# Expert down matrices loaded as four neighbouring rows per partition, in a two-block transformer kernel

## The reference, cut to what matters

```python
def expert_choice_moe(h, w_router, w1, w3, w2):
    ...
    xg = h[bidx, idx]                                  # 16 experts x 32 tokens x 1024
    h1 = jnp.einsum('becd,edf->becf', xg, w1)          # w1, w3, w2: 16 x 1024 x 1024, per layer
    h3 = jnp.einsum('becd,edf->becf', xg, w3)
    out = jnp.einsum('becf,efd->becd', jax.nn.silu(h1) * h3, w2)
    out = out * vals.astype(h.dtype)[..., None]
    return jnp.zeros_like(h).at[bidx, idx].add(out)
```

## Time and profile before

| | |
|---|---|
| median of 3 runs | 1896.9 us (1896.03 to 1896.99) |
| the profiled execution, its own time | 1900.6 us |
| its span | 1898.8 us |
| PE busy | 1550.6 us, 82% |
| PE weight loads, DVE, ACT, POOL busy | 60%, 32%, 26%, 10% |
| moved by DMA | 563.65 MB, mean 297 GB/s |
| chain that ended last | PE 52%, DMA 36% (all of it expert matrices) |

### The profile page before, as it was taken

One profiled execution on the slowest core, in us unless ns is written; L12 is line 12 of the kernel. 1 busy time (PEld: TensorE's weight loads), 2 busy tenths in 40 slices (PEclk: granted clock), 3 DMA queues, 4 the chain that ended last, 5 costly groups with the idle time before them and its releaser, 6 DMA issues.

```text
span 1898.8 us, 29516 instructions
## 1 busy us (share of the span) xinstructions
PE 1550.6 (82%) x12506; PEld 1135.1 (60%) x12506; DVE 612.3 (32%) x923; ACT 500.4 (26%) x910; POOL 193.9 (10%) x214
## 2 busy tenths in 40 slices
PE   7999999999999999665655656999998666666656
PEld 6999899998898886232322323997883322323225
DVE  3456534577556353000000002655450000000005
ACT  3433333556444432000000002454330000000003
POOL 0043000011041100000000002410100000000003
PEclk9999999999999999898888888999999888989888
DMA  8564549432554569999999999545399999999994
GB/s 284 164 219 168 195 155 301 152 111 91 178 172 136 177 233 386 425 427 424 427 426 424 427 426 377 180 152 178 128 378 394 426 425 424 427 425 427 426 425 152
DMA packets 166894, 563.65 MB, mean 297 GB/s; under 512 B 10559, under 2 KB 120027, under 8 KB 133896
## 3 DMA queue, kind: packets, MB, share of 16 engines
q1 hardware_dynamic: 159012, 552.08, 75.1%
q10 hardware_dynamic: 7780, 10.10, 1.6%
HBM read 561.08 MB, written 5.23 MB: 298 GB/s over the span
## 4 chain that ended last, share of the span: by engine, by line
PE 52%; DMA 36%; DVE 4%; ACT 3%; issue 3%; POOL 1%; SPq 0%; ACTq 0%; DVEq 0%; POOLq 0%
DMA ring<-in_moe_w 36%; PE bank L965 21%; PE bank L1213 7%; PE bank L1622 5%; PE bank L921 4%; PE bank L1060 3%; PE bank L1645 2%; PE bank L1276 2%; ACT ring_r L1695 1%; ACT big L1743 1%; PE bank L1090 1%; PE bank L1480 1%; PE bank L1285 1%; PE bank L1037 1%; PE bank L1651 1%
## 5 line engine op out<-in xcount | busy, mean ns | idle before, releaser
L1622 PE MATMUL bank<-ring,big 128*32 128x256 f32 x3840 | 281.3, 443 | 195.7 <-DMA ring<-in_moe_w 193.2
L1622 PEld LDWEIGHTS bank<-ring,big 128*32 128x32 f32 x3840 | 147.0, 123 | 335.8 <-issue 295.4
L965 PE MATMUL bank<-big_r,ring_r 128*128 128x256 f32 (+1 forms) x2760 | 344.1, 285 | 0.0
L965 PEld LDWEIGHTS bank<-big_r,ring_r 128*128 128x128 f32 (+1 forms) x2760 | 335.1, 191 | 3.0 <-issue 2.2
L2092 DVE TENSOR_TENSOR ring_r<-ring,ring_r 128x2048 fp32r<-128x2048 f32 (+2 forms) x105 | 243.0, 2319 | 135.3 <-ACT ring_r L1695 133.9
L1743 ACT ACTIVATE big<-bank 128x512 f32<-128x512 f32 (+2 forms) x186 | 87.9, 491 | 571.6 <-PE bank L921 366.8
L1695 ACT ACTIVATE ring_r<-ring 128x2048 fp32r<-128x2048 f32 (+2 forms) x109 | 204.2, 1881 | 10.4 <-DMA ring<-in_ev_w_out 5.1
L1645 PE MATMUL bank<-ring,big 128*32 128x512 f32 x1024 | 136.7, 634 | 74.0 <-DMA ring<-in_moe_w 55.5
L2479 DVE SCALAR_TENSOR_TENSOR big<-big,bank 128x256 f32<-128x256 f32 x32 | 13.5, 421 | 463.9 <-ACT big L1995 463.9
L1213 PE MATMUL bank<-ring_r,big_r 128*128 128x512 f32 x576 | 135.7, 395 | 0.7 <-DVE big_r L2099 0.7
L921 PE MATMUL bank<-big 128*128 128x128 f32 (+6 forms) x636 | 105.1, 292 | 35.7 <-ACT big L1743 18.2
(11 more groups left out here) (204 smaller groups left out, 1512.8 us busy)
## 6 DMA issues: line engine op xcount, KB each, us to landing
ring<-in_moe_w SPq DMA_DIRECT2D x120, 2048.0 KB, 23.7
ring<-in_moe_w SPq DMA_DIRECT2D x128, 1024.0 KB, 24.9
ring<-in_w_in SPq DMA_DIRECT2D x28, 1024.0 KB, 5.4
ring<-in_od_w_in SPq DMA_DIRECT2D x22, 1024.0 KB, 6.5
ring<-in_ev_w_in SPq DMA_DIRECT2D x20, 1024.0 KB, 7.3
big<-in_moe_w SPq DMA_DIRECT2D x8, 2048.0 KB, 11.2
ring<-in_ev_w_out SPq DMA_DIRECT2D x8, 1024.0 KB, 5.0
ring<-in_od_cmp_w SPq DMA_DIRECT2D x8, 1024.0 KB, 8.1
```

What stands on the lines that cost most here:

```text
L965: ins = unit[0].mark(mm(dst, lhsT, rhs, start=start and n == 0, stop=stop and n == len(terms) - 1))
L1622: ins = mm(banks[5 + up][32 * j:32 * j + 32, 0:256], xg[:, k, q, :], wv[:, r, 256 * j:256 * (j + 1)], start=k == 0, stop=k == KC - 1)
```

## The change

The down matrix of an expert is now loaded like the up matrices, in two loads of 2 MiB with 16 KB per partition. In the last expert of each batch the second of these is cut in two loads of 1 MiB, each with two neighbouring rows (8 KB) of every partition (`deep_half`). The down product takes two units, or three for that expert; its matmuls stay 16 (32 instructions), in another order. For the rows of a partition to meet their inner features, each of the four column groups of an up product now takes every fourth inner feature (`cols`) and not a block of 256 in a row, and VectorE writes `mb` straight through. Bytes, numbers of matmuls and the slots per expert stay as they are.

```diff
--- before.py
+++ after.py
@@ -784,6 +784,13 @@
                 src = flat(m)[bass.ds(row, per * P), :].rearrange("(p r) c -> p (r c)", r=per)
                 sp.dma_start(ring[:, s * SLOT:s * SLOT + per * D], src).then_inc(units_in[s], 16)
 
+            def deep_half(m, row, h):
+
+                s, rnd, n = w.next()
+                sp.wait_ge(begun, n - RING + 2 + (rnd - n // RING - 1) * RING)
+                src = flat(m)[bass.ds(row, 4 * P), :].rearrange("(p r) c -> p (r c)", r=4)
+                sp.dma_start(ring[:, s * SLOT:s * SLOT + 2 * D], src[:, 2 * D * h:2 * D * (h + 1)]).then_inc(units_in[s], 16)
+
             for l in range(LAYERS):
                 for unit in LAYER_UNITS:
                     name, i = unit[0], unit[1]
@@ -809,15 +816,19 @@
                     src = flat(ups[i % 2])[row:row + 4 * P, :].rearrange("(p r) c -> p (r c)", r=4)
                     sp.dma_start(view(spare_at[i], P, 4 * D), src).then_inc(spare_in[i], 16)
 
-                def down(row):
-                    for i in range(4):
-                        deep(a["moe_w2_2"], row + 256 * i, 2)
-
-                def expert(row):
+                def down(row, halves=False):
+                    deep(a["moe_w2_2"], row, 4)
+                    if halves:
+                        deep_half(a["moe_w2_2"], row + 512, 0)
+                        deep_half(a["moe_w2_2"], row + 512, 1)
+                    else:
+                        deep(a["moe_w2_2"], row + 512, 4)
+
+                def expert(row, halves):
                     for m in ups:
                         deep(m, row, 4)
                         deep(m, row + 512, 4)
-                    down(row)
+                    down(row, halves)
 
                 sp.wait_ge(pv_read, att_at(l, NAH + MLH))
                 spare(1)
@@ -833,11 +844,11 @@
                 deep(ups[1], first + D, 4)
                 down(first + D)
                 for q in range(2, BATCH):
-                    expert(first + q * D)
+                    expert(first + q * D, q == BATCH - 1)
                 with sp.Fori(0, NE // BATCH - 1) as b:
                     w.enter(b, BATCH * MOE_UNITS)
                     for q in range(BATCH):
-                        expert((l * NE + BATCH + q) * D + b * (BATCH * D))
+                        expert((l * NE + BATCH + q) * D + b * (BATCH * D), q == BATCH - 1)
                     w.leave(NE // BATCH - 1)
                 for name, i in PLE_UNITS:
                     tall_l(a["ple_gate_w_2"], l, D, 256 * i, 256, split=True)
@@ -1618,9 +1629,10 @@
                                 wv = U.at(P, 4, D)
                                 for r in range(4):
                                     k = 4 * part + r
+                                    cols = wv[:, r, :].rearrange("p (c j) -> p j c", j=4)
                                     for j in range(4):
                                         ins = mm(banks[5 + up][32 * j:32 * j + 32, 0:256], xg[:, k, q, :],
-                                                 wv[:, r, 256 * j:256 * (j + 1)], start=k == 0, stop=k == KC - 1)
+                                                 cols[:, j, :], start=k == 0, stop=k == KC - 1)
                                         U.mark(ins)
                             ins.then_inc(up_done, 1)
 
@@ -1636,14 +1648,18 @@
                             ins = tr(banks[7][:, r * P:(r + 1) * P], mb[:, r * P:(r + 1) * P])
                         ins.then_inc(hT_psum, 1)
                         pe.wait_ge(hT_ready, m + 1)
-                        for j in range(4):
-                            U = Unit()
-                            wv = U.at(P, 2, D)
-                            for half in range(2):
-                                for r in range(2):
-                                    c = 32 * (2 * half + r)
-                                    ins = U.mark(mm(banks[4][c:c + 32, :], hT[:, r * P + 32 * j:r * P + 32 * j + 32],
-                                                    wv[:, r, half * 512:(half + 1) * 512], start=j == 0, stop=j == 3))
+                        for part in range(2):
+                            halves = q == BATCH - 1 and part == 1
+                            for n in range(2):
+                                if halves or n == 0:
+                                    U = Unit(double=not halves)
+                                    wv = U.at(P, 2 if halves else 4, D)
+                                for half in range(2):
+                                    for r in range(2):
+                                        c, f = 32 * (2 * half + r), P * part + 32 * (2 * n + r)
+                                        ins = U.mark(mm(banks[4][c:c + 32, :], hT[:, f:f + 32],
+                                                        wv[:, r if halves else 2 * n + r, half * 512:(half + 1) * 512],
+                                                        start=part == n == 0, stop=part == n == 1))
                         ins.then_inc(down_done, 1)
                         pe.wait_ge(ob_ready, m + 1)
                         for t in range(TT):
@@ -2479,10 +2495,7 @@
                         steps.link(V.scalar_tensor_tensor(out=ma, in0=mth, scalar=1.0, in1=banks[5][:, 0:256],
                                                           op0=ALU.add, op1=ALU.mult))
                         dve.wait_ge(up_done, 2 * m + 2)
-                        done(dve, V.tensor_tensor(mb.rearrange("p (r c) -> p c r", r=2),
-                                                  ma.rearrange("p (c r) -> p c r", r=2),
-                                                  banks[6][:, 0:256].rearrange("p (c r) -> p c r", r=2), ALU.mult),
-                             act_ready, m + 1)
+                        done(dve, V.tensor_tensor(mb, ma, banks[6][:, 0:256], ALU.mult), act_ready, m + 1)
                         if q == BATCH - 1:
                             dve.wait_ge(comb_psum, m + 1)
                     steps.leave(NE // BATCH)
```

## The result

| | before | changed |
|---|---|---|
| median | 1896.47 us (1895.85 to 1896.99) | 1913.8 us (1912.38 to 1917.37) |
| ratio | | 1.0093, interval 1.0081 to 1.0106 |
| profiled execution, span | 1900.6, 1898.8 us | 1913.61, 1911.8 us |

The forecast was 1892.6 us with a range of 1890.5 to 1902. It came out as the forecast's rival C, which had 0.12.

What follows compares the result with a forecast made beforehand. It took DMA bytes to bound the expert stages, with PE's slot release mattering at their beginnings. Terms -4.3 + 0 + 0 + 0 = -4.3 us took 1896.9 to 1892.6 us; own range 1891 to 1893.5, with rivals 1890.5 to 1902.

Steps and rivals of the forecast that it cites:

- rival C: Up products at f near 2 release slots late at the start of each expert stage: 1910 us, chance 0.12.
- What bounds the stage, and the beginning as its weak place: Expert stages: DMA bytes bound the full stretch; at the beginning PE's slot release matters, 2.5 us of streaming lost.
- The loads, 0.082 us per merged pair: Down matrix loads: each merged pair saves 0.082 us, 26 pairs in each of 2 layers, 4.3 us.
- Coarser slots cost nothing: Ring slots: merged down loads wait for two slots, but no loss in full stretch or beginning; counted 0.
- The remark on the cut loads: Last expert of a batch: without its 1 MiB steps the last wait would be 2.5 us longer per layer.
- The vector step: Vector product writing mb: 421 ns instead of 600, hidden behind DMA; counted 0, bound 0.4 us for both layers.
- The up products, "I take 1.0, as nearest to a row of the same engine": Up products streaming every fourth element: slowdown factor taken as 1.0, so 0 us; other cases 1.43 and 4.
- What a factor f does: Up products slowed by f: full stretch hides up to 2.9; at stage beginnings f = 2 loses 9 us per layer.

Runs made afterwards that it cites:

- The first run above: Changed kernel with its new loads, but up products reading 256 inner features in a row again: 1893.1 us against 1899.03, ratio 0.9970.
- the third: Changed kernel with up products reading in a row in each layer's first four experts only, fourfold stride in the other twelve: 1894.75 us, ratio 0.9974.
- straight ups: Kernels with the new loads whose up products read 256 features in a row: 1893.1 us, or 1893.48 us with regrouping by eight small products behind them.
- the last experiment: Reference-computing version with straight ups and eight small products, its fp32r products reading weights at stride 2 or 4: 1907.08 us against 1899.76 for the kernel before.
- the stride alone: Kernel before with its old loads, only the up products' stream changed to every fourth inner feature: 1915.13 us, ratio 1.0081.

## Why the forecast was wrong

By its own steps:

- **What bounds the stage, and the beginning as its weak place**: right. The first run above and the third show both.
- **The loads, 0.082 us per merged pair**: right for the period, 29.36 to 29.37 us, forecast 29.34 to 29.36. The sum made of it, 4.3 us, agrees with the 5.7 measured (3.4 to 8.0), but partly by luck: inside the stages the traces show 1.1 to 2.8 us.
- **Coarser slots cost nothing**: nearly. With straight ups the beginning has 399 to 403 GB/s, as before, but the fourth expert's last MiB lands 0 to 1.2 us later. The remark on the cut loads had the wrong reason and probably the wrong size: 2.9 us in all by the medians and not 5, since the last landing doesn't move and only the work behind it doubles.
- **The vector step**: right, 422 ns; too small to be seen in the time.
- **The up products, "I take 1.0, as nearest to a row of the same engine"**: this failed. The factor was 2.07. The row that it leans on the earlier trace rows has fp32r reading elements at twice the rate of plain fp32, and I took the difference as room for a slower read. It counts elements that lie in a row, and the last experiment shows that these products have no such room: a step of 2 elements already doubles their time, 0.12 to 0.23 us. A count by 16-byte pieces would have come near the result (four elements in 4 x 0.47 ns, so one piece per 1.9 ns, while the new stream wants one per 0.86 ns, a factor of 2.2), but it is no rule either: with a step of 4 the fp32r products took one piece per 0.9 ns (0.23 us for 256). What limits the read stays open; its price is what the runs show. The Trainium skill has a rule for this (SBUF — State Buffer, in "Door 1: The DMA port swizzle"): a read that changes line with every element is penalised. Here the penalty of plain fp32 at a step of 4 is borne out, 2.07; the free step of 4 fp32 in the same note is not. The rule's other half, that two accesses in a line are enough for full rate, holds for plain fp32 at a step of 2 (0.23 us) and not for fp32r (0.23 for 0.12).
- **What a factor f does**: right in kind and in size. For f = 2 the forecast had 9 us lost per layer and releases at 742.0 and 748.9; the traces give 742.81 and 750.05, and stages 9.2 and 9.1 us longer than with the loads alone. (The 10.9 us of missing bytes of the first layer are a rougher count, by a fixed window.) For the whole it had 1910; measured 1913.8, of which some 2 us are the loads' smaller saving and the rest stays open. Up to f = 2.9 the full stretch was to hide everything, and the third experiment shows it for 2.07.

So the mechanism was on the page as a rival, with its place and nearly its price. Only the choice between f = 1 and f = 2 was wrong, and the chances were set by a row that did not measure the thing in question.

## What to carry to other kernels

Merging loads until their rows are 16 KB was worth the 0.08 us per 2 MiB that one reads from landings, and only where transfers are the bound; at the beginning of a stage the coarser loads gave a part of it back. Pay for the regrouping behind the product, where data is small (256 columns through eight small products), and not in the stream that reads the weights. A slower instruction under a stream of loads was free only while the ring is full of orders: look at the first two or three steps of the stage, where the slots come back by its pace. When a new access pattern has no row, don't price it by a row that reads elements one after another; test it alone before the change is built on it. And split a saving by stages before calling it the mechanism's: the total can hold other differences of the same size.

## What the runs showed of the hardware

- TensorE's stream of plain fp32 with a step of 16 or 64 bytes between elements takes 0.46 us per 256 columns for 0.22, with four column groups, with one of four, and on the whole array alike; a step of 8 bytes takes 0.23. In fp32r already a step of 8 bytes doubles the time, 0.12 to 0.23 us, and 16 bytes cost no more.
- One strided column group slows the other three with it: 15.01 us for four units, 14.60 with all four strided.
- Granted clock in the window of 778 to 1159: 0.98 in the changed kernel and 0.99 with the stride alone (PE busy 308 and 306 us of 381), 0.95 with three in four strided (296 us), 0.84 to 0.88 with straight ups (234 to 250 us). At a stage's end the difference was 1.8 us in the first layer: last MiB and scatter at 0.50 and 0.55 in the kernel before, at 1.00 in the changed one.
- Two loads of 1 MiB in 8 KB rows took 0.08 us more of a full stream than one of 2 MiB in 16 KB rows: an expert's period went from 29.52 to 29.36 us.
